# A hybrid decoder trunk: its S5 layer by chunks of four state tiles, channels on partitions, norm weights on turned rows

## What is computed

```python
h = rmsnorm(x, norm_mix_g[1])
xr = einsum('bsgc,gpc->bsgp', u, bbr); xi = einsum('bsgc,gpc->bsgp', u, bbi)   # u: h in 64 groups of 16
_, _, sr, si = lax.associative_scan(combine, (a_r, a_i, xr, xi), axis=1)       # s = a * s_before + x, complex
y = einsum(sr, c_re) - einsum(si, c_im) + d_skip * h
g = gelu(y)
x = x + g * sigmoid(g @ glu_w + glu_b)
# experts: idx and gate from two top-16 searches and a top-16 of their sums
act = gelu(einsum('td,tkd->tk', h, u_tab[idx]))
x = x + einsum('tk,tkd->td', gate * act, v_tab[idx])
```

## Time and profile before

| | |
|---|---|
| median of 3 runs | 1639.1 us (1638.93 to 1649.3) |
| profiled execution | 1638.64 us |
| its span | 1636.5 us, 15247 instructions |
| read from HBM over the span | 605.19 MB |

### The profile page before, as it was taken

How to read it: one execution, slowest core, us unless ns; L and a number is a source line. 1 busy time by engine, 2 the same in 40 slices (tenths; PEclk the granted TensorE clock), 3 DMA queues, 4 the chain that set the end, 5 groups by cost and what they waited for, 6 DMA issues and landing times. The chain is left out here.

```text
span 1636.5 us, 15247 instructions
## 1 busy us (share of the span) xinstructions
PE 1365.2 (83%) x3816; PEld 623.7 (38%) x3816; DVE 1141.5 (70%) x2821; ACT 759.3 (46%) x2074; POOL 588.8 (36%) x517
## 2 busy tenths in 40 slices
PE   7999789888597888787989788887898988777776
PEld 3544334333242343443444344444434432222222
DVE  2337865657656989998565799898865476666764
ACT  2324542544334756654353655656433354444443
POOL 0025233344233343353332344344333254443441
PEclk9999899999799899998999998999799999999999
DMA  9569999989699999899999998989899899999996
GB/s 359 189 244 388 395 380 391 405 354 417 266 413 417 390 361 347 346 375 364 354 415 411 416 415 331 347 336 375 308 399 416 320 416 421 422 421 422 421 421 254
DMA packets 106406, 607.22 MB, mean 371 GB/s; under 512 B 9296, under 2 KB 9424, under 8 KB 40784
## 3 DMA queue, kind: packets, MB, share of 16 engines
q0 software_dynamic: 73728, 536.90, 81.6%
q1 hardware_dynamic: 32592, 69.37, 11.5%
HBM read 605.19 MB, written 1.05 MB: 370 GB/s over the span
## 5 line engine op out<-in xcount | busy, mean ns | idle before, releaser
L869 PE MATMUL ps<-rings,dgs 128*128 128x512 f32 x2048 | 1006.3, 632 | 217.3 <-ACT dgs L626 216.8
L434 POOL DMA_INDIRECT rings<-in_uv_tab_dram,idx x512 | 587.5, 1147 | 981.5 <-PE ps L869 886.7
L1264 DVE CUSTOM_DVE_ANT_0 rings<-rings,h 128x1024 f32<-128x1024 f32 x512 | 614.0, 1223 | 163.5 <-DMA rings<-in_uv_tab_dram,idx 146.7
L869 PEld LDWEIGHTS ps<-rings,dgs 128*128 128x128 f32 x2048 | 387.5, 199 | 768.8 <-ACT dgs L626 385.9
L620 ACT ACTIVATE gel<-dots 128x1 f32<-128x1 f32 x512 | 102.8, 201 | 567.3 <-DVE dots L1264 557.5
L626 ACT ACTIVATE dgs<-cst,wgt 128x128 f32<-128x128 f32 x512 | 205.5, 401 | 37.2 <-issue 2.5
L676 PE MATMUL ps<-wst,hT 128*128 128x512 f32 x384 | 179.2, 605 | 9.7 <-DMA wst<-in_wq_dram 7.3
L623 ACT ACTIVATE wgt<-gel,share 128x1 f32<-128x1 f32 x512 | 150.8, 295 | 37.4 <-issue 2.8
L676 PEld LDWEIGHTS ps<-wst,hT 128*128 128x128 f32 x384 | 73.8, 195 | 102.7 <-issue 101.2
L1041 DVE COPY mem<-ps 128x512 f32<-128x512 f32 x16 | 11.1, 691 | 108.3 <-PE ps L668 108.3
L620 ACT ACT_TABLE_LOAD x56 | 71.8, 1283 | 1.7
(11 more groups left out here) (173 smaller groups left out, 893.6 us busy)
## 6 DMA issues: line engine op xcount, KB each, us to landing
wst<-in_wq_dram SPq DMA_DIRECT2D x15, 2048.0 KB, 19.4
wst<-in_w_out_dram SPq DMA_DIRECT2D x4, 2048.0 KB, 19.7
rings<-in_uv_tab_dram,idx POOLq DMA_INDIRECT x512, 10.5
wst<-in_glu_w_dram SPq DMA_DIRECT2D x4, 2048.0 KB, 26.7
rings<-in_w_in_dram SPq DMA_DIRECT2D x3, 2048.0 KB, 16.6
vec<-in_vecs_dram SPq DMA_DIRECT2D x11, 512.0 KB, 11.4
rings<-in_w_in_dram SPq DMA_DIRECT2D x2, 1024.0 KB, 8.7
dgs<-in_w_in_dram SPq DMA_DIRECT2D x1, 2048.0 KB, 19.4
```

Of the source, the lines that this page charges most:

```text
L434: nc.gpsimd.indirect_dma_start(out=ring[:, g % RING, :], out_offset=None, in_=uv_tab, in_offset=bass.IndirectOffsetOnAxis(ap=idx[n % 4][:, ...
L869: ins = PE.matmul(ps[:, 4 + 2 * t + b, :], diag[:, g % DIAGS, :], ring[:, g % RING, D + b * BANK:D + (b + 1) * BANK], start=(g % (PH * TOP ...
L1264: V.tensor_tensor_reduce(out=u, in0=u, in1=h[:, t, :], scale=1.0, scalar=0.0, op0=ALU.mult, op1=ALU.add, accum_out=dots[n % 2][:, s:s + 1] ...
```

## The change

- **S5 by chunks.** A chunk of four state tiles is one unit, one every 11 slots from slot 10. One rotation of 1024 elements, sums of 512, and one scan for the four tiles' real and one for their imaginary parts: the decay lies in a tile that ScalarE fills (`s5_decay`), with a zero at each tile's first time step, and the carry of the second token tile is added to the first step's input.
- **Output turned round.** C is stationary (32 columns) and the states move (128 columns), so channels lie on partitions; D is a diagonal matrix (`one_diag`) in a product of its own, and the bias a product of a row of ones with a row of 1024. Gelu then writes the operand of the GLU product at once; the gate is transposed only for the last product.
- **Norm weights on turned rows.** For the four mixing norms `norm_h` goes. Norms 0 and 1 turn raw x, and 1/rms goes into the rotary tables and the scale of `z_out`; norms 4 and 6 turn x by a product with a diagonal of 1/rms. The weights, one column per 128 channels (`cols`), are applied in `hT_copy`.
- **Loads.** `load_vec` has three loads in place of eleven, in one buffer; `cols` (96 bytes a partition) and a row of 4 KB per token tile (`load_row`) are new. The ring of diagonals for the experts has 8 entries in place of 16.

```diff
@@ between, for each token tile
-        norm(g, 3, 4 + 2 * t)
-        for pair in range(S5_TILES // 2):
-            slot = 9 + 5 * pair
-            at(g, slot, ("s5_mm", t, pair))
-            at(g, slot + 1, ("s5_rot", t, pair))
-            at(g, slot + 2, ("s5_turns", t, pair))
-            at(g, slot + 3, ("s5_scan", t, pair))
-            at(g, slot + 4, ("s5_tables", t, pair))
-        at(g, 89, ("s5_last", t))
-        at(g, 90, ("s5_sum", t))
-        at(g, 91, ("s5_gelu", t))
-        at(g, 92, ("gate_T", t))
-        at(g, 93, ("gT_copy", t))
+        mix_norm(g, 3, 4 + 2 * t)
...
+        for c in range(KC):
+            slot = 10 + 11 * c
+            at(g, slot, ("s5_in", t, c), ("s5_decay", t, c))
+            at(g, slot + 1, ("s5_rot", t, c))
+            at(g, slot + 2, ("s5_add", t, c))
+            at(g, slot + 3, ("s5_scan", t, c))
+            at(g, slot + 4, ("s5_cmat", t, c))
+            at(g, slot + 5, ("s5_back", t, c))
+            if c + 1 < KC:
+                at(g, slot + 3, ("s5_turns", t, c + 1))
+                at(g, slot + 4, ("s5_frac", t, c + 1))
+                at(g, slot + 6, ("s5_tables", t, c + 1))
+            at(g, slot + 7, ("s5_out", t, c))
+            if c % 4 == 3:
+                at(g, slot + 8, ("s5_gelu", t, c // 4))
@@ ScalarE
+            def s5_decay(t, c):
...
+                A.activation(decay[:, :, 1:P], dec[:, 4 * c:4 * c + 4].unsqueeze(2).to_broadcast([P, 4, P - 1]),
+                             ACT.Copy).then_inc(dt5_ok, 1)
@@ TensorE
+                PE.matmul(ps[:, bank, cols_], one_diag[:, :], hTs[t][:, c, :], start=True, stop=False)
+                terms = ((by_cos, 0, 0), (by_sin, 1, 1), (by_sin, 0, 2), (by_cos, 1, 2))
+                for q, (z_, r, v) in enumerate(terms):
+                    for j in range(4):
+                        ins = PE.matmul(ps[32 * j:32 * j + 32, bank, cols_], m[:, j, v, :], z_[:, r, j, :],
+                                        start=False, stop=(q == 3))
...
+                    PE.matmul(ps[:, 2 + b, :], one_row, glu_row[:, b * BANK:(b + 1) * BANK], start=True, stop=False)
@@ VectorE
+            def s5_scan(t, c):
+
+                dve.wait_ge(dt5_ok, KC * t + c + 1)
+                for r in range(2):
+                    w = by_cos[:, r, :, :].rearrange("p j s -> p (j s)")
+                    ins = V.tensor_tensor_scan(w, decay.rearrange("p j s -> p (j s)"), w, 0.0, ALU.mult, ALU.add)
```

More of the change, by code:

```diff
@@ L106, in norm, with mix_norm @@
                 at(n, slot + i, (name, m))
+    def mix_norm(n, slot, m):
+        for i, name in enumerate(("norm_sq", "norm_ms", "norm_sd", "norm_r", "norm_d", "norm_T", "hT_copy")):
+            at(n, slot + i, (name, m))
     def product(n, slot, name, *which):
@@ L271, in trunk @@
         turns, whole = part(4864, 512, a=4), part(5376, 512, a=4)
-        prod = [[part(5888 + 1024 * i + 512 * v, 512, "p (i r s) -> p i r s", i=2, r=2) for v in range(2)]
-                for i in range(2)]
-        zst = part(7936, 512, "p (i r s) -> p i r s", i=2, r=2)
+        by_cos, by_sin = (part(5888 + 1024 * v, 1024, "p (r j s) -> p r j s", r=2, j=4) for v in range(2))
+        decay = part(7936, 512, a=4)
         bs = part(2816, 2048, "p (c r j g n) -> p c r j g n", c=8, r=2, j=4, g=2)
@@ L840, in s5_mm @@
                     banks_2_3()
[L841 to L853 removed]
+                if ci >= 2:
+                    pe.wait_ge(w_ok, ci - 1)
@@ L855, in glu_mm, with gate_T @@
+            def gate_T(t, b):
+                pe.wait_ge(g_ok, 2 * t + b + 1)
+                for a in range(4):
+                    ins = PE.transpose(ps[:, b, a * P:(a + 1) * P], hTs[t][:, 4 * b + a, :], ident)
+                ins.then_inc(gT_done, 1)
             def glu_mm(t, b, k0, k1):
+                pe.wait_ge(g_ok, 2 * t + 1 + (k1 > 4))
+                use = GLU_USE[t] + b
+                w = block_of(use)
                 if k0 == 0:
-                    pe.wait_ge(gT_act, t + 1)
@@ L900, in norm_ms, with norm_r @@
                 V.tensor_scalar(ms[:, t:t + 1], ss[:, t:t + 1], 1.0 / D, RMS_EPS, ALU.mult, ALU.add).then_inc(ms_done, 1)
+            def norm_r(m):
+                t = NORM_T[m]
+                dve.wait_ge(sd_done, m + 1)
+                V.reciprocal(rstd[:, t:t + 1], sd[:, t:t + 1]).then_inc(r_ok, 1)
+                dve.drain()
+                if m < 2:
+                    dve.wait_ge(ld_cst, 16)
+                    for w in (cos_t, sin_t, nsin_t):
+                        V.tensor_scalar(w[:, t, :], w[:, t, :], rstd[:, t:t + 1], None, ALU.mult)
+                    dve.drain()
             def norm_h(m):
@@ L1142, in s5_rot @@
                 dve.drain()
-            def s5_scan(t, pr):
-                c, js, cos, sin, by_cos, by_sin = s5_views(pr)
-                for i in range(2):
-                    tile = 4 * c + js.start + i
-                    for r in range(2):
-                        V.tensor_tensor_scan(zst[:, i, r, :], dec[:, tile:tile + 1].to_broadcast([P, P]), by_cos[:, i, r, :],
-                                             z_init[:, r, tile:tile + 1] if t else 0.0, ALU.mult, ALU.add)
+                if t == 1:
+                    V.tensor_tensor(by_cos[:, :, :, 0], by_cos[:, :, :, 0], z_last[:, :, 4 * c:4 * c + 4], ALU.add)
+                    dve.drain()
@@ L1155, in s5_scan, with s5_back @@
                 if t == 0:
-                    tile = 4 * c + js.start
-                    V.tensor_copy(z_last[:, tile:tile + 2, :], zst[:, :, :, P - 1])
+                    V.tensor_copy(z_last[:, :, 4 * c:4 * c + 4], by_cos[:, :, :, P - 1])
+            def s5_back(t, c):
+                cos, sin = s5_tabs(KC * t + c)
+                V.tensor_tensor(by_sin, by_cos, sin, ALU.mult).then_inc(d_ok, 1)
                 dve.drain()
-                if pr % 2 and pr + 1 < 16:
-                    fraction(KC * t + c + 1)
@@ L1184, in glu_sum @@
[L1184 to L1190 removed]
+                V.tensor_tensor(by_cos, by_cos, cos, ALU.mult).then_inc(d_ok, 1)
```

382 lines of the change are left out of this document (188 added, 194 removed).

## The result

The changed kernel takes 1668.4 us (median of 4 runs, 1663.5 to 1674.8) against 1641.6 us for the one before beside it: a ratio of 1.018 with a 95% interval from 1.014 to 1.021. It is 1.8% slower where 2.7% faster was forecast (the interval is clear of no change, but reaches 2%). The profiled execution spans 1666.2 us, 29.7 more than before.

What follows compares the result with a forecast made beforehand. VectorE was taken to bound the S5 stretches, transfers or TensorE the rest; -21.5 - 21 + 5.2 - 2 - 4 = -43.3 us gave 1595 us against 1639.1. Likeliest case 1575 to 1612, all cases 1562 to 1624.

Steps and rivals of the forecast that it cites:

- the term of waits in the 84 slots: Expert slots beside S5: most of 8.9 us of VectorE waits goes, gather waits stay 4.5, 3 us added for late transfers.
- The 84 slots: Expert slots run beside S5, per token tile: 246.5 us falls to 225, and 250.6 falls by 21.
- Waits for gathers: VectorE ahead of the dot products in the S5 stretch: 4.5 us of waits, taken to stay.
- S5 prices on VectorE: VectorE's S5 work per chunk of four tiles: 10.9 us becomes 9.5, with a scan of 512 at 1.12 us.
- Waits as work: Rival 1's doubt that ScalarE blocks and low-clock stretches may be part of what was counted as VectorE work.
- TensorE's outputs: S5 outputs per chunk on TensorE: 34 instructions at 0.12 us each, 4.1 us, hidden behind VectorE.
- Rival 3: TensorE becomes the bound in the S5 stretch: outputs at 0.43 us an instruction, 1674 us in all; chance 0.06.
- GLU stretch: Four slots behind the 84, bound by TensorE: bias products and transposes add 2.6 us per token tile, to 24 us.
- Start: Kernel start: raw x turned on landing and one load gone before the weights; 0.5 to 2.7 us saved, 2 taken.
- Loads: Fewer broadcast vector loads: seven not yet counted, worth 0 to 8.8 us together, 4 taken.
- Norms: Two norms of 1.28 us leave VectorE: priced at nothing, at most 2.6 us less.
- Rival 2: Queues do not mesh in the 84 slots: waits of 9% add 12 us per token tile, 1619 us; chance 0.12.

Runs made afterwards that it cites:

- e1: The changed kernel with the S5 inputs of every chunk but the first put five slots earlier on TensorE; 1595.3 us, ratio 0.975.
- e8: The kernel before the change, with the next chunk's fraction and tables made five slots earlier, after the even pair; 1622.1 us, ratio 0.991.
- e6: The kernel before the change, with loads 2 to 9 of the eleven vectors cut to eight columns; 1634.0 us against 1639.1, ratio 0.9977.
- e5: e1 with the two scans of 512 elements of each chunk taken apart into eight of 128; 1594.0 us, ratio 0.972.

## Why the prediction was wrong

**The step that failed** is the term of waits in the 84 slots: "Waits: the tables are now made six slots ahead of use, not one, so most of the 8.9 goes; the waits for gathers stay at 4.5". It counted one edge between engines into VectorE's rotation, the tables, and put the other, TensorE's inputs, at nothing without a reason. The order rows showed it: TensorE's inputs (L813, ahead of the outputs of the pair before) became a row behind the expert block of their own slot (L853), and the table of stages put them in the slot ahead of the rotation. The prediction took each distance in slots of one shared counter, as if the engines stood at the same slot. They don't: when VectorE reaches a rotation, TensorE is 1.5 to 5.75 slots behind. The new wait is 76.3 us, 37.2 and 39.1 in the two stretches; with the lead given back they take 36.6 and 38.2 us less, and the kernel 1595.3 us. That 1595 was forecast is in part luck: the terms below are off in both directions, and the four runs spread from 1585 to 1603.

- *What bounds the stretch:* right. VectorE ends last there; e1 has 2 us of waits in 221.
- *The 84 slots:* 225 and 229.6 forecast, 257.8 and 262.2 measured, 221.2 and 224.0 without the new wait.
- *Waits for gathers:* the 4.5 us ahead of the dots were misread. They are short gaps, only 0.5 of them a listed wait, and none for a gather; the 2.2 us ahead of the copy of the transposed gate (L1175), also in the 84 slots, were left out.
- *S5 prices on VectorE:* right. Scans of 512 take 1.21 us (1.1 to 1.2 forecast). By start-to-start steps, with waits left out, a chunk takes 9.4 and 9.6 us in e1 where 9.5 was forecast, and 11.0 and 11.3 before (10.9). Between e8 and e1 the 84 slots differ by 19.5 and 16.1 us; without the listed waits 13.1 and 12.6, where the forecast has 13.6 (11.2 for the chunks, 2.4 for the tail).
- *Waits as work:* the 8.9 us at L1137 were table waits and went, as forecast. That part of the gain did not need the chunks: e8 has it, 14 us, in the kernel before.
- *TensorE's outputs:* priced too high, on the safe side. 34 instructions were priced at 4.1 us; they take 1.3 (below). Rival 3 is out.
- *GLU stretch:* the size is right, the place is not. +2.6 was forecast for each token tile, and slots 94 to 107 show +2.7 and +2.4; but the first four, where it was to make 24 us, take 17.4 and 17.1 where they took 21.2, and the nine behind them 6.6 more. This is TensorE from the last outputs on:

```profile
802.57 0.38 PE L865 MATMUL ps<-hT,one_diag 128*128 128x128 f32 x2
802.89 1.08 PE L869 MATMUL ps<-mem 128*32 128x128 f32 x32
803.90 1.98 PE L902 MATMUL ps<-rings,dia 128*128 128x512 f32 x4
805.81 1.12 PE L889 MATMUL ps<-mem,cst 1*128 1x512 f32 x2
806.87 3.70 PE L891 MATMUL ps<-wst,hT 128*128 128x512 f32 x8
...
815.55 0.60 PE L877 MATMUL ps<-cst,hT 128*128 128x128 f32 x4
...
827.98 10.58 PE L902 MATMUL ps<-rings,dia 128*128 128x512 f32 x24
```

L889 is the bias (1.12 for one), L877 the transpose; VectorE's four waits at L1216 (35.1 us; the counterpart L1182 had 26.6 before) come behind this chain, by way of ScalarE.
- *Start:* -2 forecast, -1.0 to the first dot product and -1.2 to the first gather:

```profile
4.55 1.97 PE L690 MATMUL ps<-cst,x 128*128 128x128 f32 x8 [4.55 <-DMA cst<-in_cst_dram]
8.97 23.55 PE L698 MATMUL ps<-rings,hT 128*128 128x512 f32 x48 [2.45 <-DMA rings<-in_w_in_dram]
32.37 1.04 PE L690 MATMUL ps<-cst,scr 128*128 128x128 f32 x8
```

The first gather of the same trace:

```profile
100.65 1.08 POOL L448 DMA_INDIRECT rings<-in_uv_tab_dram,idx  x1 [60.77 <-DVE idx L1277]
```

TensorE starts 4 us sooner, then waits 2.45 for weights, so that the products start 2.3 us sooner. They take 23.55 us, not 22.54: six of their instructions take 0.85 us or more to the next, where three did before and a fourth 0.80, and nearly all others 0.43. These slow steps end at 14.23 us of the span in one kernel and at 14.80 in the other. The prediction had this as the lower end of its term; PEclk reads 1.00 over these microseconds, so no row shows that it was the clock.
- *Loads:* 4 us forecast; e6 has 4, with 0.5 to 7 possible. The phase-0 slots of the changed kernel show 1.1.
- *Norms:* priced at nothing; slots 0 to 10 take 1.8 and 2.4 us more (in e1 -0.2 and +2.4, so the first isn't firm). Turning x by a product takes 16 instructions and here 2.51 us where the transposes of h took 8 and 1.04 (each 8 blocks). Part of it is the clock, granted at 0.77 over this row; in e1, granted in full, the same 16 take 1.95:

```profile
535.38 2.51 PE L726 MATMUL ps<-one_diag,x 128*128 128x128 f32 x16
```

Rival 2 named the right family, queues that do not mesh, and was given 0.12 and 12 us for each token tile; the new wait is 37 and 39. Its argument against, eight gather buffers that absorb 20 us, works the other way here: the slack of the buffers lets TensorE fall behind. It named no place, so its price had no source: the place was one edge with one slot of distance.

## What to carry to other kernels

Where several engines walk one list of places, a distance in places is not a distance in time. For every edge between two engines, take the lag of the one behind from the trace (here dots started less experts started when VectorE passes, up to 5.75) and ask for as many places as that, above all on the edge into the engine that bounds the stage. Look for the longest lag behind blocks of a third engine that both depend on, as ScalarE's tables here. When a change merges small units into large ones, check that each producer's lead was carried over; a lead hidden in a line such as "inputs of the next pair" is lost without a trace in the work counted.

## What the runs showed of the hardware

Outputs in four column strips, 128 rows by 32 columns stationary and 128 columns moving, take 1.08 us for 32 instructions, 34 ns each, though the profile's group gives a mean of 276 ns for one: strips run beside each other. At the 0.12 that an output took before, 32 would be 3.9 us, so the gain is some 3.6 by this estimate. The Trainium skill, "TensorE: Matmul & The Clock Gate", Part 3, has a measured gain of 2.38 for three column tiles; the row points the same way. Its sentence that weight loads overlap only where the row group differs would have made them dearer, and the rows go against it: all strips use all rows, and 32 loads with a mean of 109 ns each lie within 0.81 us.

```profile
802.89 0.81 PEld L869 LDWEIGHTS ps<-mem 128*32 128x32 f32 x32
```

The inputs show the same for row strips: 16 instructions in 0.73 us, where 8 in blocks of two strips took 0.72.

The fixed part of a VectorE instruction was small: 48 scans more in a stretch cost 2.3 us of busy time (e5), 0.05 us each, less than the 0.08 forecast and far from the 0.16 that follows from the errata section of "VectorE: DVE Perf Modes" in the Trainium skill. The duration of a single row does hold such a 0.16 (0.69 us for 512 elements at 1.04 ns), but the next instruction starts 0.61 us after it.
